# Hybrid decoder layer: compressed attention in 16 steps with the selection inside, and another order of query tiles in sparse attention

## The reference, cut to what matters

```
kc, vc = compress_tokens(...)                 # 127 blocks of 32 tokens, stride 16
s = q . kc * scale - slope * dist             # compressed: distance to a block's end
p_cmp = masked_softmax(s, valid) * any(valid)
o_cmp = p_cmp . vc
imp = sum over the group's heads of (p_cmp . a_sel)   # 32 blocks of 64 tokens
imp = FORCED for block 0, the current and the one before; -1 for later ones
idx = top_k(imp, 8)                           # selection, per group and query
o_sel = masked_softmax(q . ks[idx] ..., tok <= t) . vs[idx]
o_win = masked_softmax(q . kw ..., 0 <= t - k < 512) . vw
out = g0 * o_cmp + g1 * o_sel + g2 * o_win    # sigmoid gates per query and head
```

## Time and profile before

| | us |
|---|---|
| median of 3 runs | 3399.29 (3396.03 to 3399.51) |
| the profiled execution's own time | 3396.3 |
| its span, first to last instruction | 3394.3 |
| compress, 984 to 1044 | 60 |
| compressed attention, 1044 to 1175 | 131 |
| selection and scaling, 1175 to 1214 | 39 |
| sparse attention, 1214 to 2003 | 789 |
| PE / DVE / ACT / POOL busy over the span | 2988.0 / 1369.5 / 998.8 / 556.2 |
| granted TensorE clock, mean | 0.939 |

### The profile page before, as it was taken

One profiled execution on the slowest core, in us unless ns is written; L12 is line 12 of the kernel. 1 busy time (PEld: TensorE's weight loads), 2 busy tenths in 40 slices (PEclk: granted clock), 3 DMA queues, 4 the chain that ended last, 5 costly groups with the idle time before them and its releaser, 6 DMA issues. The chain is left out here.

```text
span 3394.3 us, 37684 instructions
## 1 busy us (share of the span) xinstructions
PE 2988.0 (88%) x13210; PEld 1759.8 (52%) x13211; DVE 1369.5 (40%) x3249; ACT 998.8 (29%) x2050; POOL 556.2 (16%) x564
## 2 busy tenths in 40 slices
PE   8999999999977658989999969999699899859990
PEld 5544444444447644545665646666544355446670
DVE  3421212111214555555565648888511111152236
ACT  1100000000005524544555536666411012113332
POOL 0121100111003430131311220000121100001116
PEclk9999999999988869999999989999899999869995
DMA  3212111121142220011111020110364333625848
GB/s 119 77 60 71 68 68 56 68 71 68 56 117 78 79 86 27 6 61 34 57 41 47 7 95 1 38 38 1 131 217 141 139 124 124 272 64 204 322 166 309
DMA packets 120754, 323.41 MB, mean 95 GB/s; under 512 B 13216, under 2 KB 49696, under 8 KB 112416
## 3 DMA queue, kind: packets, MB, share of 16 engines
q1 hardware_dynamic: 100320, 247.54, 20.6%
q0 software_dynamic: 14096, 51.39, 4.5%
q10 hardware_dynamic: 6192, 22.55, 1.6%
HBM read 206.42 MB, written 115.02 MB: 95 GB/s over the span
## 5 line engine op out<-in xcount | busy, mean ns | idle before, releaser
L305 PE MATMUL p_ps<-token_sums,p_ws 128*128 128x512 f32 x768 | 340.0, 592 | 0.0
L305 PEld LDWEIGHTS p_ps<-token_sums,p_ws 128*128 128x128 f32 x768 | 145.9, 190 | 183.7 <-issue 183.7
L305 PE MATMUL p_ps<-xnT,p_w 128*128 128x512 f32 x512 | 233.0, 598 | 5.2 <-PEq L59 5.2
L1704 PE MATMUL o_ps<-o_w,o_mT 128*128 128x512 f32 x512 | 224.0, 596 | 14.0 <-DMA o_w<-in_w_out 14.0
L314 ACT ACTIVATE p_kept<-p_ps 128x512 f32<-128x512 f32 x32 | 19.1, 598 | 737.3 <-PE p_ps L305 737.3
L1054 PE MATMUL b_po<-b_probT,vsw 128*64 128x256 f32 (+1 forms) x1824 | 232.0, 376 | 0.0
L327 DVE TENSOR_TENSOR p_kept<-p_ps,p_kept 128x512 f32<-128x512 f32 x96 | 66.4, 692 | 391.5 <-PE p_ps L305 391.5
L1130 DVE CUSTOM_DVE_ANT_0 b_prob_s<-b_pq,b_sel 128x896 f32<-128x896 f32 (+5 forms) x192 | 167.8, 911 | 134.6 <-PE b_pq L1013 125.8
L1296 PE MATMUL d_pq<-d_keys,d_q 64*128 64x512 f32 (+3 forms) x640 | 185.4, 578 | 28.1 <-DVE d_seg_max L1401 15.8
L1013 PE MATMUL b_pq<-ks,b_q 64*128 64x512 f32 (+3 forms) x688 | 166.2, 542 | 40.4 <-DVE b_seg_max L1130 26.4
L1401 DVE CUSTOM_DVE_ANT_0 d_prob<-d_pq,d_bias 128x1024 f32<-128x1024 f32 (+6 forms) x192 | 168.0, 910 | 65.9 <-PE d_pq L1296 63.1
(11 more groups left out here) (278 smaller groups left out, 4766.9 us busy)
## 6 DMA issues: line engine op xcount, KB each, us to landing
projT<-p_stage SPq DMA_DIRECT2D x128, 256.0 KB, 2.3
y<-e_y ACTq DMA_DIRECT2D x43, 512.0 KB, 4.3
p_w<-in_wt SPq DMA_DIRECT2D x16, 1024.0 KB, 5.5
gates_T<-projT SPq DMA_DIRECT2D x16, 1024.0 KB, 10.0
wgu<-in_w_gu SPq DMA_DIRECT2D x4, 4096.0 KB, 15.6
y<-m_zeros POOLq DMA_DIRECT2D x20, 512.0 KB, 11.8
p_xin<-in_x SPq DMA_DIRECT2D x16, 512.0 KB, 3.7
mergedT<-m_stage SPq DMA_DIRECT2D x8, 1024.0 KB, 11.6
```

What stands on the lines that cost most here:

```text
L305: mm = nc.tensor.matmul(ps[n % 8][:], weights[:, k, :], moving[:, k, :], start=(k == 0), stop=(k == HK - 1))
L1704: mm = nc.tensor.matmul(ps[b][k][:], mT[:, b, dt, :], w[:, dt, k * 512:(k + 1) * 512], start=(dt == 0), stop=(dt == DT - 1))
```

## The change

1. **Queries scaled once.** `t_projection` multiplies the results of the four query pairs by `qscale` on ScalarE before they are stored; the scaling on POOL in `sparse_attention` goes.
2. **Compressed attention in 16 steps.** One unrolled block with steps (chunk c, head pair i), both groups in a step. All 4 MB of queries, the distances and the constants are loaded in `compress`, behind the other loads; TensorE and VectorE wait for all five constants. Only 32(c + 1) columns of `kc` are used. The distance is added by VectorE out of PSUM, and the slope enters as ScalarE's scale; sums are VectorE's reductions. The gate is multiplied into the probabilities, so that the value product gives the gated output already turned (`ycT`), stored from `y`. POOL multiplies by the rate and adds up over head pairs.
3. **Selection inside.** A chunk's sum is turned in step 4c + 5, multiplied with `overlap` at 4c + 6 and its blocks chosen at 4c + 7; the function `selection` goes.
4. **Sparse attention.** The "C" flats go: the compressed output is fetched by DMA into `y` two units ahead. `PAIR_ORDER` becomes 4, 3, 5, 2, 6, 1, 7, 0.

The core of the diff:

```diff
@@ t_projection
+            sp.dma_start(qscale[:], d["nsa_qscale"]).then_inc(qscale_in, 16)
...
+                if 2 * j < PAIRS:
+                    for n, tile, half in RESULTS:
+                        act.wait_ge(summed, 7 * q + n)
+                        x = stage[:, q % 2, 2 * tile + half, :]
+                        nc.scalar.activation(x, x, ACT.Copy, scale=qscale[:, 2 * j + tile:2 * j + tile + 1]).then_inc(q_scaled, 1)
@@ compress, sync block, behind vsw, ks and kw
+            for o, n in ((s.cmp_dist, "cmp_dist"), (s.cmp_valid, "cmp_valid"), (s.cmp_slope, "cmp_slope"), (s.overlap, "overlap")):
+                sp.dma_start(o[:], d[n]).then_inc(s.cmp_const_in, 16)
+            for c in range(NCH):
+                cols = slice(c * 512, (c + 1) * 512)
+                sp.dma_start(s.q[:, :, cols], d["qkT"][0:PAIRS, :, cols].rearrange("i p c -> p i c")).then_inc(s.q_in[c], 16)
+            sp.dma_start(s.keep_force[:], d["sel_keep_force"]).then_inc(s.cmp_const_in, 16)
-            nc.gpsimd.memset(s.pbar[:], 0.0)
@@ compressed_attention, POOL
+                rate = stat[:, n % 4, 3].unsqueeze(3).to_broadcast([P, GROUPS, 4, w])
+                pool.wait_ge(rate_ready, n + 1)
+                    nc.gpsimd.tensor_tensor(plain[:, :, :, 0:w], prob[n % 4][:, :, :, 0:w], rate, ALU.mult).then_inc(plain_ready, 1)
+                    pool.wait_ge(plain_ready, n - c)
+                    nc.gpsimd.tensor_tensor(acc, acc, plain[:, :, :, 0:w], ALU.add).then_inc(summed, 1)
@@ compressed_attention, TensorE
+                for j in range(4):
+                    t = (4 * c + j) * P
+                    for g in range(GROUPS):
+                        rows = slice(g * HD, (g + 1) * HD)
+                        mm = nc.tensor.matmul(pq[n % 2][:, g, j, 0:w], s.q[rows, i, t:t + P], s.kc[rows, 0:w], start=True, stop=True)
+                    mm = nc.tensor.matmul(po[g * HD:(g + 1) * HD, :], s.vc[:, g * HD:(g + 1) * HD], probT[:, n % 2, g, :], start=True, stop=True)
+            pe.wait_ge(s.cmp_const_in, 80)
+            scores(0)
+            scores(1)
+            for n in range(LAST):
+                if n + 2 < NS:
+                    scores(n + 2)
+                if n < NS:
+                    pe.wait_ge(gate_done, n + 1)
+                    turn(gated[n % 2], step_use[n])
+                if 1 <= n <= NS:
+                    values(n - 1)
+                if n in sel_turn:
+                    turn(pbar[c % 2], sum_use[c])
+                if n in sel_product:
+                    importance(sel_product[n])
@@ compressed_attention, ScalarE
+                        op = nc.scalar.activation(x, x, ACT.Exp, bias=stat[:, n % 4, 1, g, j:j + 1], scale=slopes[PAIRS * g + i])
+                nc.scalar.activation(y[:, n % 2, :], po[:], ACT.Copy).then_inc(evicted, 1)
@@ compressed_attention, VectorE
+                nc.vector.tensor_tensor(x, pq[n % 2][:, :, :, 0:w], away, ALU.add).then_inc(added, 1)
+                nc.vector.tensor_reduce(stat[:, n % 4, 0], x, AX.X, ALU.max).then_inc(maxed, 1)
+                nc.vector.scalar_tensor_tensor(out=stat[:, n % 4, 1], in0=stat[:, n % 4, 0], scalar=0.1 * NEG if c == 0 else 2 * NEG,
+                                               in1=s.cmp_slope[:, i], op0=ALU.max, op1=ALU.mult).then_inc(neg_ready, 1)
...
+                link(nc.vector.tensor_reduce(total, x, AX.X, ALU.add))
+                    nc.vector.reciprocal(rate, total).then_inc(rate_ready, 1)
+                link(nc.vector.tensor_tensor(weight, rate, by, ALU.mult))
+                nc.vector.tensor_tensor(gated[n % 2][:, :, :, 0:w], x, weight.unsqueeze(3).to_broadcast([P, GROUPS, 4, w]), ALU.mult).then_inc(gate_done, 1)
@@ selection, sync and POOL blocks
-            pool.wait_ge(s.b_const_in, 32)
-            for k in range(2):
-                scale_queries(nc, pool, s, k)
@@ sparse_plan, sparse_attention
-PAIR_ORDER = [0, 7, 1, 6, 2, 5, 3, 4]
+PAIR_ORDER = [4, 3, 5, 2, 6, 1, 7, 0]
-        flats += [(u, "W", 2 * p + 1, (1,)), (u, "R", 0, (0, 1)), (u, "C", 0, (0, 1))]
+        flats += [(u, "W", 2 * p + 1, (1,)), (u, "R", 0, (0, 1))]
+            def load_compressed(u):
+                p, i = units[u]
+                if u >= 2:
+                    sp.wait_ge(stored[u % 2], 16 * (u // 2))
+                sp.dma_start(y[:, u % 2, :], d["ycT"][i][:, p * 2 * P:(p + 1) * 2 * P]).then_inc(ya_in[u % 2], 16)
-                    scale_queries(nc, pool, s, k + 1)
                     mask(k + 1)
```

493 lines of the change are left out of this document (225 added, 268 removed).

## The result

The changed kernel takes 3307.64 us (median of 4 runs, 3306.21 to 3309.19) where the kernel before takes 3399.4 (4 runs, 3396.03 to 3402.62): a ratio of 0.973, 95% interval 0.9713 to 0.9747. Its profiled execution took 3306.2 us with a span of 3304.1, against 3396.3 and 3394.3.

What follows compares the result with a forecast made beforehand. TensorE bounds sparse attention; no engine bounds compressed attention, which loses time restarting between rounds. Compressed stage 2 + 7 + 118 + 9 + 2 = 138 against 170.4 (−32), sparse attention −21: 3396.3 − 53 → 3343 us, range 3316 to 3370.

Steps and rivals of the forecast that it cites:

- TensorE's time per step: Compressed attention: 7.6 us a step at half clock, 9.0 with selection work, 3.8 and 4.5 at full clock.
- VectorE's step: Compressed attention: 3.4, 5.4, 6.8, 8.4 us by chunk, with the gating multiply held by POOL's multiply.
- Ahead and the tail: Compressed stage: 9 us before the steps (constants 2, first step 7), 11 after the last gate (9, clearing 2).
- (a): Sparse attention: 32 transposed pairs of compressed outputs go, 0.31 us each as TensorE has no gaps: −9.9 us.
- (b): Start of sparse attention: first masks take 12 us for 14.5, so −2.5 us.
- (c): Sparse attention's new pair order: −12 us at the start, +3 against it, so −9, bounds +5 and −15.
- The wait of about 7 us behind POOL's mask ahead of pair 7: Sign expected in sparse attention: a gap of about 7 us, as pair 1 before 7 meets a longer mask.
- R1: Full clock in compressed attention's steps: they take 102 us, total 3327, down to 3310; chance 0.20.
- R2: Half clock throughout compressed attention's steps: 138 us, total 3363, or 3370 without most of the order's gain; chance 0.17.
- R4: Compressed attention's steps don't overlap: some 290 us in a row instead of 118, total 3515; chance 0.05.
- R5: Waits inside compressed attention's steps give the restarts back, sparse attention unchanged: within 7 us of 3396; chance 0.04.
- R3: Sparse attention's new order gives nothing and the masks take as long as before: 3355; chance 0.12.

Runs made afterwards that it cites:

- pool_later: Changed kernel with POOL's multiply by the rate waiting until VectorE's gating multiply ends: 3297.13 us, ratio 0.9696.
- scores_full: Changed kernel with only the score products of compressed attention on all 128 columns: 3301.28 us, ratio 0.9709.
- order_alone: Kernel before with only the new pair order 4, 3, 5, 2, 6, 1, 7, 0: 3394.84 us, ratio 0.9982.
- c_slot: Changed kernel with a nearly empty third turned part per sparse attention unit (one transpose, one-column copy, own place in the schedule): 3326.0 us, ratio 0.9781.
- c_back: Changed kernel with the third turned part back in each sparse attention unit (two transposes, ScalarE copy, own place), unread: 3326.81 us, ratio 0.9783.
- c_copy: Changed kernel with an extra ScalarE copy of 256 columns per sparse attention unit, no transposes or place: 3313.95 us, ratio 0.9742.

## Why the prediction was wrong, point by point

**What bounds the kernel, and where the time would come from**: right. Both stages named gained, the rest moved by 2 us, and the steps overlap.

**The step that failed is TensorE's time per step** ("3.5 + 2.0 + 2.1 = 7.6 at the half clock, so the clock decides"). The term that was mis-sized is the score products: I took them from 128-row products of 32 columns in selection, 0.22 us a record; the new ones have 64 rows, and 16 records took 1.92 us, 0.12 each. (The new selection products, 128 rows as those of before, took 3.62 us for 16 records at the half clock: the old price is right for the old kind.) Transposes and values were as priced (1.97 and 1.98). So TensorE needs 5.9 us a step at the half clock and not 7.6, and with the half clock gone at about 1062, VectorE sets the steps from chunk 1 on. Chunks 0 and 1 took 32.3 us for the 56 I gave them: 24 of the 37 us that the forecast missed. The price of the products is not all of that. In chunk 0 (14.0 for 30) it is 1.7 us a step, about 7. The gating multiplies there start 3.0, 4.0 and 6.2 us apart: only the last of these is a step with all of TensorE's work, as the first three steps' scores were made ahead and no values were due, and 16 steps have 15 distances where I charged 16. These two make the other 9 us. In chunk 1 (18.3 for 26) the half clock that I had mixed in was gone, 4 us by my own price for VectorE, and VectorE's step was shorter than that price, 3 us. That the clock would be at half in chunk 0 was right, and that it decides held there only: the 6.2 us step has 2.7 us of waiting for score products. Behind it, kept at 1.00 from 1065 on, it gives 1.9 us. The Trainium skill (TensorE: Matmul & The Clock Gate, Part 1) has the throttled state as the default and activity as what releases it. The rows agree in direction: the clock falls behind the pauses at the choices and stays up where unread products fill them. In chunk 0 TensorE was busy 5.00 of 5 us twice in a row at 0.50 before it rose, so a busy engine alone did not mean the full clock at once; and in sparse attention it fell from 1533 to 1540 with TensorE busy for all of the 7 us.

**VectorE's step.** The mechanism was right and its size a little high: 4.0, 5.5 to 6.0, 7.0 us where I had 4.6, 6.0, 7.6 without the choice. A small operation follows the next within 0.2 us in all, and POOL's multiply holds the gating multiply for 0.31, 0.74, 1.16, 1.59 us (by pool_later's lengths) instead of 0.6 to 2.0. The choice (3.4 us, the first at 1083.95) was as priced, but only two of the four fall in the steps; the others lie in the tail, where VectorE waits. Chunk 3 was 6 us shorter than forecast, chunk 2 by 1.

**Ahead and the tail.** Constants were not waited for (first scores at 1043.54), and the lead was 4 us shorter. The tail was 9 longer: I priced the chain of the last sums and left out what stands before it in TensorE's queue (selection products of chunk 2, values of two steps with one PSUM buffer) and the last choice itself. That the choice was "counted" does not hold: the steps' 0.8 us stands in chunks 1 to 3 only, three choices for four. I also took the 16 records of the selection products at 1.8 us, where the sum for TensorE's step has 3.5; the last ones took 1.97. And the clock, at 0.59 on the mean, makes 3.4 and 4.5 us of it against pool_later and scores_full, whose mean is 0.81 and 0.83.

**Sparse attention.** (a) Priced at 9.9 as TensorE time; 18.0, of which the transposes are 5 to 7 and the rest its place in the schedule, with pair 7's late mask the largest part. "TensorE has no gaps there" is where it broke: it has, and where they fall depends on the count of flats. (b) The masks: 14.46 to 11.86, forecast 2.5, measured 2.6. (c) The order: 4 to 5 us in the stages and 6 to 8 by the ratios, where I had 9; right in sign, and near in size only by luck, two errors that cancel (24 for 12 saved by pair 0 last, 20 for 3 given back; single traces, so each with the spread named above). The 3 did not follow from its own terms either: a wait of 7 for one of 8.48 is a gain. Not foreseen in it: the longer start, +4.7. The wait of about 7 us behind POOL's mask ahead of pair 7 did not come in the changed kernel, but narrowly. POOL starts that mask as soon as the distances land, ends it at 1722.20, and VectorE takes it at 1723.08:

```profile
1708.26 13.94 POOL L921 TENSOR_TENSOR b_sel<-b_sel,sel_mask 128x1920 f32<-128x1920 f32 x4 [0.50 <-DMA b_sel<-in_dist]
```

With slightly other timing the wait is there: 8.46 us in order_alone, 9.15 in c_slot, 5.91 in c_back, 4.75 in c_copy. So the mechanism was right, and the changed kernel missed the wait by 0.9 us; by the traces of order_alone and c_back, 6.8 us went with the scaling on POOL and the other loads, which I had put at nothing. The first of pair 7's units are 36.1 to 36.6 us apart, as forecast.

**The rivals.** R1 (full clock) came nearest with 3327 down to 3310, but for another reason: the clock is 0.76 on the mean of the stage, and it is VectorE's shorter steps, the cheap products and the light start of chunk 0 that make 87 us of its 102. R2, R4 and R5 fell with the stage at 112. R3 (the order gives nothing) fell with order_alone.

## What to carry to other kernels

Take the price of a product from one with the same number of rows, and before letting the clock decide, ask which engine sets the step at either clock: where VectorE does, the half clock costs next to nothing (1.9 us with the pauses filled), and where TensorE's chain ends last, as at the end of the stage, it costs 3 to 5 (15.4 to 17.9 us at a mean clock of about 0.8, 19.9 and 22.7 at 0.59 and 0.50). In a schedule written in cycles, a removed operation is worth its place as well as its time, so price it by the length of units with and without such a place, and look in the units that changed most for one wait that does it. Before a difference of a few us between two traces is given a cause, compare it unit by unit, and look at the clock in the units that differ. At the end of a stage, list everything in the engine's queue ahead of the last piece, and look there for an idle engine that can do the next stage's first work: that, with POOL's multiply started behind the gating multiply instead of with it, brought 15 us more.
